# An image sweep with its low parts on VectorE and four buffers for fetched rows, in a two-block transformer kernel

## The reference, cut to what matters

```
def block(hb):                      # 128 tokens at a time
    q = (hb @ w_q).reshape(128, 8, 2, 256)
    s = einsum("nhkd,hkmd->nhkm", q, sub_keys)
    s_half, i_half = top_k(s, 16)
    cand = s_half[:, :, 0, :, None] + s_half[:, :, 1, None, :]
    top_s, top_c = top_k(cand.reshape(128, 8, 256), 16)
    ids = k1 * 128 + k2             # 8 heads x 16 experts for each token
    g = softmax(top_s)
    ue, ve = u_tab[ids], v_tab[ids]
    act = gelu(einsum("nd,nhkd->nhk", hb, ue))
    return einsum("nhk,nhkd->nd", g * act, ve)
```

## Time and profile before

| what | value |
|---|---|
| median of the runs | 4207.81 us |
| the profiled execution's own time | 4205.89 us |
| its span, first to last instruction | 4204.1 us |
| mean granted TensorE clock | 0.898 |
| PE matmul busy | 3324.1 us, 79% |
| DVE (VectorE) busy | 3015.6 us, 72% |
| ACT (ScalarE) busy | 1238.8 us, 29% |
| POOL (GpSimd) busy | 998.4 us, 24% |
| DMA | 824.28 MB, mean 196 GB/s |

### The profile page before, as it was taken

One profiled execution on the slowest core, in us unless ns is written; L12 is line 12 of the kernel. 1 busy time (PEld: TensorE's weight loads), 2 busy tenths in 40 slices (PEclk: granted clock), 3 DMA queues, 4 the chain that ended last, 5 costly groups with the idle time before them and its releaser, 6 DMA issues.

```text
span 4204.1 us, 52606 instructions
## 1 busy us (share of the span) xinstructions
PE 3324.1 (79%) x18426; PEld 2778.2 (66%) x18426; DVE 3015.6 (72%) x4973; ACT 1238.8 (29%) x1924; POOL 998.4 (24%) x731
## 2 busy tenths in 40 slices
PE   6996879677890037878977777777698999999998
PEld 3685778556770025778866556555576988888887
DVE  0179744546974479598689999999856798777776
ACT  1214400103410002208422222222233346444443
POOL 0002212223313310000266666666540000000000
PEclk8998978889995568989998888888899999999999
DMA  7544625667856667621678888888664523555554
GB/s 260 200 135 156 205 75 170 216 224 248 284 199 187 180 187 233 208 93 53 197 261 258 262 260 260 262 260 261 227 166 155 176 91 126 191 190 191 191 190 155
DMA packets 246971, 824.28 MB, mean 196 GB/s; under 512 B 40704, under 2 KB 50960, under 8 KB 245536
## 3 DMA queue, kind: packets, MB, share of 16 engines
q1 hardware_dynamic: 136864, 493.41, 35.7%
q0 software_dynamic: 85632, 319.43, 23.7%
q10 hardware_dynamic: 24320, 9.37, 0.9%
HBM read 797.80 MB, written 23.27 MB: 195 GB/s over the span
## 4 chain that ended last, share of the span: by engine, by line
PE 35%; DVE 30%; DMA 11%; issue 10%; ACT 1%; POOL 0%; DVEq 0%; SPq 0%; ACTq 0%; POOLq 0%
PE psum L1324 10%; DMA work<-in_u_rows,H 6%; PE psum L1310 6%; DVE arena L2346 6%; DMA stage<-in_u_rows,H 4%; PE psum L1312 3%; DVE u_split L2916 3%; PE psum L1429 3%; PE psum L742 2%; DVE work L2323 2%; DVE coef_split L2929 2%; DVE work L2921 1%; PE psum L1003 1%; PE psum L1292 1%; DVE arena L2838 1%
## 5 line engine op out<-in xcount | busy, mean ns | idle before, releaser
L1324 PE MATMUL psum<-v_split,coef_split 128*128 128x512 f32 x2856 | 797.3, 435 | 247.2 <-DVE coef_split L2930 221.2
L1324 PEld LDWEIGHTS psum<-v_split,coef_split 128*128 128x128 f32 x2856 | 585.0, 211 | 403.1 <-DVE coef_split L2930 251.0
L1310 PE MATMUL psum<-input_split,u_split 128*128 128x512 f32 x1856 | 660.1, 394 | 0.0
L1312 PE MATMUL psum<-input_split,u_split 128*128 128x256 f32 x1856 | 524.6, 283 | 0.0
L569 POOL DMA_INDIRECT arena<-in_v,arena x256 | 337.1, 1317 | 335.7 <-DVE arena L2346 278.9
L1310 PEld LDWEIGHTS psum<-input_split,u_split 128*128 128x128 f32 x1856 | 353.2, 190 | 76.8 <-DVE u_split L2916 0.2
L2001 ACT ACTIVATE work<-work 128x256 f32<-128x256 f32 x232 | 97.1, 418 | 1003.8 <-DVE work L2921 1003.8
L1312 PEld LDWEIGHTS psum<-input_split,u_split 128*128 128x128 f32 x1856 | 355.0, 191 | 11.7
L2930 DVE TENSOR_TENSOR coef_split<-work,coef_split 128x256 fp32r<-128x256 f32 x256 | 325.0, 1269 | 8.7
L1721 ACT ACTIVATE arena<-psum 128x1024 f32<-128x1024 f32 (+5 forms) x192 | 156.3, 821 | 586.6 <-PE psum L1254 294.5
L2346 DVE SCALAR_TENSOR_TENSOR arena<-arena 128x1024 f32<-128x1024 f32 x254 | 314.5, 1285 | 12.1 <-DMA arena<-in_v,arena 12.1
(11 more groups left out here) (492 smaller groups left out, 5633.5 us busy)
## 6 DMA issues: line engine op xcount, KB each, us to landing
ring<-in_w SPq DMA_DIRECT2D x420, 512.0 KB
ring<-in_u SPq DMA_DIRECT2D x256, 512.0 KB
ring<-in_v SPq DMA_DIRECT2D x256, 512.0 KB
scratch_inj<-arena ACTq DMA_DIRECT2D x16, 512.0 KB, 3.3
arena<-scratch_inj POOLq DMA_DIRECT2D x7, 1024.0 KB, 8.4
arena<-in_keys POOLq DMA_DIRECT2D x3, 2048.0 KB, 11.2
scratch_cm<-work POOLq DMA_DIRECT2D x8, 512.0 KB, 5.9
scratch_cm<-arena POOLq DMA_DIRECT2D x8, 512.0 KB, 3.5
```

What stands on the lines that cost most here:

```text
L1310: mm(bank(b), rows[:, 0, P * k:P * k + P], HR[:, k, :, :], start=(k == 0), stop=False, skip_group_check=True)
L1312: last = mm(bank(b)[:, 0:S], rows[:, 1, P * k:P * k + P], HR[:, k, 0, :], start=False, stop=(k == 7), skip_group_check=True)
L1324: last = mm(bank(2 + 2 * i + f), CFR[:, b, c, P * i:P * i + P], parts[:, v, 512 * f:512 * f + 512], start=(first and c == 0 and v == 0), s ...
```

## The change

The diff, cut to its core:

```
-UBUFS, VBUFS = 2, 4
-FIRST_PICK, LAST_PICK = 27, NEXP - 3
-DOTS = {"in": 24, "misc": 7, "inverse": 3, "levels": 12, "recurrence": 23, "attention": 22, "merge": 8,
-        "add": 14, "up": 44, "down": 10}
+UBUFS, VBUFS = 4, 4
+FIRST_PICK, LAST_PICK = 15, NEXP - 3
+VROWS_FREE = (6, 10, 18, 26)
+DOTS = {"in": 24, "misc": 7, "inverse": 4, "levels": 12, "recurrence": 9, "gated": 18, "attention": 25, "merge": 8,
+        "add": 14, "up": 44, "down": 21}
+def pick_buffers():
+    uses, last, out = [0] * VBUFS, [None] * VBUFS, []
+    for j in range(FIRST_PICK, LAST_PICK + 1):
+        ready = [b for b in range(VBUFS) if VROWS_FREE[b] < j - 1]
+        for m in range(picks_until(j - 1), picks_until(j)):
+            b = min(ready, key=lambda b: -1 if last[b] is None else last[b])
+            out.append((b, uses[b], last[b]))
+            uses[b], last[b] = uses[b] + 1, m
+    return out
...
# u rows: two more buffers, at an address in the arena that changes from stage to stage
+ROW_HOMES = {"in": 14336, "misc": 14336, "inverse": 14336, "levels": 14336, "recurrence": 27648, "gated": 18432,
+             "attention": 18432, "merge": 18432, "add": 18432, "up": 14336, "down": 9728, "rest": 6144}
...
# GpSimd, fetch_u: waits for a home that is new in its stage; and the calls
+    if place == "recurrence": pool.wait_ge(sem("level_masked"), LEVELS - 1)
+    if place == "gated":      pool.wait_ge(sem("gdn_out"), 1)
+    if place == "down":       pool.wait_ge(sem("ffn_inner"), 1)
+    if place == "rest":       pool.wait_ge(sem("inputs_scaled"), 3 * KD_)
-fetch_u(dots_until("inverse") - 2)
+fetch_u(dots_until("misc") + UBUFS)
-    fetch_u(dots_until("inverse") + 2 * lev - 2)
+    fetch_u(dots_until("inverse") + 2 * lev - 2 + UBUFS)
...
# GpSimd, sweep p = 0: the low parts of v are gone, the fetches remain
-    pool.tensor_tensor(parts[:, 1, :], ring[:, w % RING, :], parts[:, 0, :].bitcast(F32), ALU.subtract)
+for m, (b, k, last) in enumerate(PICKS):
+    if last is None:
+        pool.wait_ge(sem("coef_ready"), VROWS_FREE[b])
+    else:
+        pool.wait_ge(sem("rows_used"), NFETCH + last + 1)
+    pool.indirect_dma_start(VROWS[b], None, v_rows, ...ROW_IDS2[:, m:m + 1]...)
...
# TensorE, split tiles of "in" and "up": banks 0 to 3 take turns
-    pe.wait_ge(sem("lin_free"), l0 + t - 1)
+    pe.wait_ge(sem("lin_free"), max(l0 + t - 3, l0 - PLAIN))
# TensorE, up of the sweep, p = 0: three products of 256 columns for each k
+    for x, w in ((0, 0), (1, 0), (0, 1)):
+        last = mm(bank(b)[:, 0:S], rows[:, w, P * k:P * k + P], HR[:, k, x, :], ...)
...
# ScalarE, p = 0: GELU reads PSUM; the coefficient's cast
+    act.wait_ge(sem("up_ready"), j + (n0 + 1))
+    act.wait_ge(sem("coef_ready"), j + (n0 - 1))
+    f(AC[:, b, :], bank(b)[:, 0:S], ACT.Gelu_apprx_tanh)
+def coef_high(j, b):
+    act.wait_ge(sem("gated"), j + (2 * KD_ - e - 1))
+    act.wait_ge(sem("coef_used"), j + (n0 - 1))
+    copy(CFR[:, b, 0, :], CT[:, b, :]).then_inc(sem("coef_high"), 1)
# ... called in the order gelu(j), high_u(j+2), coef_high(j), high_v(j+1); and, outside the sweep,
# ScalarE waits for the dots that use a home before it writes there (three places)
# VectorE, steady loop of p = 0
+    low(1, j, b, w0 + 2 * j + 2)
+    dve.wait_ge(sem("gelu_done"), j + 1)
+    tt(CT[:, b, :], AC[:, b, :], G[:, j, :], ALU.mult).then_inc(sem("gated"), 1)
+    if made["picks"] < some:
+        pick()
+    dve.wait_ge(sem("coef_high"), j - e - 1)
+    tt(CFR[:, b, 1, :], CT[:, b, :], CFR[:, b, 0, :].bitcast(F32), ALU.subtract).then_inc(sem("coef_ready"), 1)
+    low(0, j + 2, b, w0 + 2 * j + 3)
+    while made["picks"] < some:
+        pick()
```

More of the change, by code:

```diff
@@ L84, in dots_until, with dot_place @@
             return n
+def dot_place(n):
+    for name in DOTS:
+        if n < dots_until(name):
+            return name
+def pick_buffers():
[7 more added lines that the diff above has]
+    return out
 def picks_until(j):
@@ L548, in _ @@
             unpark(KEPT_BACK, kept, 2)
[L549 to L558, removed]
+            for m, (b, k, last) in enumerate(PICKS):
+                if m == picks_until(NEXP - 9):
                     pool.wait_ge(sem("coef_ready"), NEXP - 10)
@@ L1305, in up @@
                     rows = u_parts(b, early)
-                    if not first:
-                        pe.wait_ge(sem("sum_ready"), j + (s0 - e - 1))
+                    if not first and p == 0:
+                        pe.wait_ge(sem("gelu_done"), j + (n0 - 1))
+                    elif not first:
+                        pe.wait_ge(sem("sum_ready"), j - e - 1)
                     pe.wait_ge(sem("u_low"), j + (s0 - e + 1))
                     for k in range(8):
+                        if p == 0:
+                            for x, w in ((0, 0), (1, 0), (0, 1)):
+                                last = mm(bank(b)[:, 0:S], rows[:, w, P * k:P * k + P], HR[:, k, x, :],
+                                          start=(k == 0 and not x and not w), stop=(k == 7 and w == 1))
+                            continue
                         mm(bank(b), rows[:, 0, P * k:P * k + P], HR[:, k, :, :], start=(k == 0), stop=False,
@@ L1910, in _ @@
             for t in range(16):
+                if t == 8:
+                    act.wait_ge(sem("rows_used"), dots_until("levels"))
                 one(lambda ps: f(GB[:, t, :], ps[:, 0:S], ACT.Sigmoid))
@@ L1938, in _ @@
             root(R1[:, 0:S], R2[:, 0:S])
+            act.wait_ge(sem("rows_used"), dots_until("add"))
             input_high(2)
@@ L2664, in _ @@
             L.give(cp(OG[:, :, P:S], PS(3072, 8, P)), "gdn_out")
-            dots("recurrence", 8)
+            dots("gated", 12)
             L.take("rowsum")
@@ L2669, in _ @@
             others(8)
-            dots("recurrence", 6)
+            dots("gated", 6)
             L.take("heads_spread")
@@ L2699, in _ @@
                 sc, SH = PS(1024, 4, 512), SC[:, h, :]
-                dots("attention", 5 if half == 0 else 2)
+                dots("attention", 8 if half == 0 else 3)
                 L.take("scores_ready")
@@ L2713, in _ @@
                 SH = SC[:, h, :]
-                dots("attention", 4)
+                dots("attention", 5 + half)
                 L.take("probs_exp")
@@ L2723, in _ @@
                 gdn_out(2)
-            dots("attention", 7)
+            dots("attention", 3)
             L.take("attention_out")
@@ L2758, in _ @@
             L.lin += FT
+            dots("down", 6)
             def parameters():
@@ L2860, in _ @@
                 next(par, None)
-                dots("down", 2 if t < 5 else 0)
+                dots("down", (4, 5, 1, 1, 1, 1, 1, 1)[t])
                 if t == 6:
@@ L2874, in _ @@
                 L.mark(tt(H[:, k, 0:S], X[:, k, 0:S], R2[:, 0:S], ALU.mult), "inputs_scaled")
+            dots("rest")
             prepare_lags(1)
-            dots("rest")
             assert made["dots"] == NFETCH, made
@@ L2969, in split_experts @@
                                 steady(i * 2 + (j0 + b), b)
-                total(NEXP - 2, 0)
-                if p:
-                    low(1, NEXP - 2, 0, w0 + 2 * NEXP - 2)
-                coef(NEXP - 2, 0)
-                if p:
-                    low(1, NEXP - 1, 1, w0 + 2 * NEXP - 1, closing=True)
-                total(NEXP - 1, 1)
-                coef(NEXP - 1, 1)
+                for j in (NEXP - 2, NEXP - 1):
+                    if p:
+                        total(j, j % 2)
+                    if j == NEXP - 2:
+                        low(1, j, 0, w0 + 2 * j + 2)
+                    coef(j, j % 2)
+                    if j == NEXP - 2:
+                        low(1, NEXP - 1, 1, w0 + 2 * NEXP - 1, closing=True)
                 dve.wait_ge(sem("coef_used"), n0 + NEXP)
```

79 lines of the change are left out of this document (43 added, 36 removed).

## The result

The changed kernel takes 3676.45 us (3664.65 to 3677.12, four runs) against 4207.51 us (4207.11 to 4215.97) of the kernel before: a ratio of 0.873 with a 95% interval of 0.871 to 0.875, or 531 us less. The forecast was 3831 us, 375 us less, with a range from 3720.

The account below looks back on a forecast made before the run. No engine bounds the whole kernel; in the sweep VectorE, slowed by lockout with GpSimd, sets the pace, then DMA. Gains 175 + 126 + 32 + 9 + 20 + 9 + 4 = 375 us; 4206 - 375 = 3831 us, range 3720 to 3970.

Parts of the forecast that it names:

- The mechanism in the sweep: Image sweep: VectorE and GpSimd lock each other out, about 2.2 us per expert; the coefficient's low part falls to 0.43 us.
- Rival (c): Sweep: lockout comes from GpSimd's indirect fetches and stays; 8.9 us per expert, 14 us lost there, 4020 us total; chance 0.05.
- (d): Sweep: VectorE without pause keeps GpSimd from issuing fetches; an expert takes 13.4 us, 4521 us total, slower; chance 0.03.
- the term of 7.2 us per expert: Sweep, experts 15 to 126: DMA limits an expert to 7.2 us at 313 GB/s, bounds 6.3 and 8.0; 175 us gained.
- a share over 0.9: Sweep: DMA share over 0.9 at 7.2 us per expert was to show the forecast; 0.8 with VectorE busy throughout, (a).
- VectorE's 6.28 us per expert: Sweep: VectorE's work per expert after the change, with two low parts, gate product, coefficient's low part and 2.306 picks.
- the 16 us that I added for the thin start and the pause: Sweep: 8 us for few free row buffers in experts 15 to 27, 8 for GpSimd bringing X back near the end.
- rival (a): Sweep: VectorE stays the bound, DMA delivers 360 GB/s; 6.4 us per expert, 264 us gained, 3742 us total; chance 0.17.
- Levels: Inversion levels: fetches called four ahead remove TensorE's 32.1 us wait; 32 us gained, 26 to 46.
- "rest": Stage of 70 remaining dots: four buffers are no limit, 1.9 us per dot (1.5 to 2.3); 126 us gained (98 to 154).
- Are the dots free in "down"?: Stage "down" gets 11 more dots, 6 of them in a 9.93 us VectorE idle gap; cost 0, at worst 10 us.
- The other stages: Gains ahead of L2676 9 us, attention 20, "add" 9, "up" 4, "inverse" 2, "in" 0; four PSUM banks worth nothing.

## Why the prediction was wrong, by its steps

**The mechanism in the sweep: right.** The coefficient's low part went to 0.418 us and no 3 us ones are left. Moving the one subtraction gives 206 us alone and its undoing costs 114. Rival (c) is refuted by the changed kernel, where only the fetches remain on GpSimd and VectorE is not held, and (d) by 5.98 us per expert.

**The step that failed: "DMA ... This is where the gain stops", the term of 7.2 us per expert.** An expert takes 5.98 us, and VectorE sets its pace, not DMA. I had divided the rate by the busy share (254/0.79, 281/0.83) and called the result, 321 to 338 GB/s, the rate at share 1. The runs show 379 GB/s at 1.00 and 406 at 1.02, and TensorE never waits for a transfer at 406. Busy share does not scale with the rate: at 0.81 DMA had moved 260 GB/s before, and 285 in the run with half of the fetches. Even the bounds were off, as 6.3 us was the low end. The trace of the kernel before could have told: in its first 100 us it has short stretches, of plain loads, far above 338 GB/s:

```profile
78.00:88.00 10.00, 5.06 (x32) 3.62 (x30) 0.17 (x1) 0.77 (x2) 0.00 (x0) 0.92 1.01 412
2.00:22.00 20.00, 9.35 (x40) 4.83 (x40) 5.46 (x13) 4.51 (x12) 0.00 (x0) 0.90 0.97 367
```

The Trainium skill's figure (DMA: Bandwidth & Descriptors, section "Specifications", about 358 GB/s for a core) is exceeded as well, by the long rows with 373, 379 and 406 GB/s; this kernel runs on one core. The sign that I had named for DMA as the bound, a share over 0.9, came too (1.00), though VectorE was the bound: it could not tell the two apart.

**VectorE's 6.28 us per expert: too long by 0.5.** I added durations (1.22, 0.44, 0.43, 1.286). In the run with half of the fetches, where little else holds it up, the expert takes 5.78. From start to start the same instructions are 1.14, 0.34, 0.34 and 1.20 us: 2 x 1.14 + 0.34 + 0.34 + 2.306 x 1.20 = 5.73. With VectorE's idle time of 17.7 us in the 75 experts of 450 us, 0.24, that makes the 5.98 us measured to 0.01. The prediction's own rows for two low parts had no starts next to each other; a timeline would have shown them. With 5.98 instead of 7.2, 111 experts are 136 us less; the 16 us that I added for the thin start and the pause came out as 27 (12 and 15), which leaves the 126 missed. So the likeliest case should have been rival (a), and even that (3742) had the durations in it.

**Levels: 32 forecast, 54 measured, more than the upper bound of 46.** The wait was sized rightly from TensorE's 32.1 us. The rest, which I had only in that bound, is the clock: 0.73 from 545 to 610 us where TensorE waits once per level and 1.00 where it doesn't. Five steps from level to level, from one L1134 to the next (L1111 before), took 120.1 us and take 62.2: 57.9 less, 32.1 of it waiting and 25.8 slower products. The late-fetch run gives 53 us of the stage back.

**"rest": right in size.** 1.93 us per dot for 1.9, 125 us for 126. The reason was only half right, so the close number is in part luck: GpSimd is busy for 87 of 134 us there and DMA moves 277 GB/s at 0.83; no resource is full. VectorE waits 52 us for landings. A landing takes 5.5 us (median from the issue) and 4.3 in the run with two buffers, where a dot takes 2.94: so I read the 1.93 as four buffers with a turn of 7.7 us, which the prediction had at 5.7. More than four were not tried.

**Are the dots free in "down"?** No. The table's 8 us hide the 6.9 us of `prepare_lags(1)` that left this stage. From the last dot of "up" to the product that makes H it was 95.8 us and is 105.7, 9.9 lost, all of the 10 that I allowed as the worst; and then VectorE waits 4.9 us for the first row of "rest". The first line is of the kernel before:

```profile
1250.83 2.77 DVE L2874 TENSOR_TENSOR H<-X,work 128x256 f32<-128x256 f32 x8 [0.55 <-ACT work L1739]
```

```profile
1142.17 2.77 DVE L2919 TENSOR_TENSOR H<-X,work 128x256 f32<-128x256 f32 x8 [0.55 <-ACT work L1769]
1149.87 1.22 DVE L2369 SCALAR_TENSOR_TENSOR arena<-arena,X 128x1024 f32<-128x1024 f32 x1 [4.92 <-DMA arena<-in_u_rows,H]
...
1284.08 1.16 DVE L2883 TENSOR_TENSOR arena<-arena 128x960 f32<-128x960 f32 x1
```

**The other stages:** 10 for 9, 16 for 20, 13 for 9 (merge and add); "up" 13 for 4, in to inverse 13 for 2. In attention the wait that was 14.7 us is 0.7, as forecast, but the one for the softmax only fell from 18.5 to 17.2 where I had 6:

```profile
PE psum L1232 <- DVE arena L2765: 17.2, 2, 10.6
...
PE psum L765 <- DVE arena L2770: 0.7, 1, 0.7
```

I had taken VectorE's busy share (144 of 156 us) as a bound of 12 on "up"; the gain needed that bound in full. Why "in" to "inverse" gained 13 was not looked into. The four banks gave nothing, as said.

## What to carry to other kernels

Look for the fastest stretches with several transfers in flight, short ones too, and don't divide a rate by its busy share: they give a rate that the limit is not below (412 GB/s in 10 us here, against the 321 to 338 that I had worked out); if no stretch asks for more than it gets, write the limit down as unknown and let the range reach to the next engine's bound. Sum an engine's work from start to start in a timeline, not by durations. And when two engines hold each other up, moving the work to the busier one can be the gain: price it as the locked-out time less the work moved (1.16 us against the 1.07 measured), and look for waits beside it that go too (2.15 us measured on the kernel before).

## What was not expected of the hardware

- DMA on one core: 379 GB/s over 450 us with ring loads and gathered 4 KB rows mixed, 406 GB/s with VectorE relieved, where TensorE's pace asked for no more.
- An indirect fetch on GpSimd takes 0.94 us beside an idle VectorE, 1.75 beside one pick and 2.01 beside a VectorE without gaps. It was hidden here, with 2.3 of them in 6.0 us.
- Seven us of filler products in an 8.2 us wait raised the granted clock from 0.71 to 0.84 only; the products behind the last 1.17 us of idle time still ran partly at half clock.
